# Two layers on one core: earlier chunk loads around a second weight, transposes in place of products, and constant products in TensorE's first gaps

## The reference

```
h = rms_norm(x, g)                          # both layers begin so
p = h @ w_in_2                              # 2048 x 6448
wd, ad, gd, a, b = the narrow parts of p    # 304 columns: "LoRA" inputs, decay and beta
...
L = where(strict, (k_beta @ k.T) * gamma, 0)        # 8 heads x 4 chunks of 64 tokens: 32 of 64x64
sol = triangular_solve(L + eye, [v_beta, k_beta * exp(g)])
```

## Time and profile before

| | |
|---|---|
| median of 3 runs | 2945.02 us |
| the profiled execution | 2943.11 us, its span 2941.4 us |
| PE (matmul) busy | 2876.3 us, 98% |
| PEld (weight load) | 2480.6 us, 84% |
| DVE (VectorE) busy | 1600.7 us, 54% |
| ACT (ScalarE) busy | 1167.7 us, 40% |
| POOL (GpSimd) busy | 58.6 us, 2% |
| DMA | 501.12 MB, mean 170 GB/s |

### The profile page before, as it was taken

How to read it: one execution, slowest core, us unless ns; L and a number is a source line. 1 busy time by engine, 2 the same in 40 slices (tenths; PEclk the granted TensorE clock), 3 DMA queues, 4 the chain that set the end, 5 groups by cost and what they waited for, 6 DMA issues and landing times.

```text
span 2941.4 us, 41822 instructions
## 1 busy us (share of the span) xinstructions
PE 2876.3 (98%) x18274; PEld 2480.6 (84%) x18274; DVE 1600.7 (54%) x1325; ACT 1167.7 (40%) x958; POOL 58.6 (2%) x124
## 2 busy tenths in 40 slices
PE   8999999999999999999998999988899999999998
PEld 7999888888888888888888989988788888888887
DVE  5657555444554455444447657875555445544445
ACT  4345444334443333333335343423344343333333
POOL 0000000000000000002002000000000000000000
PEclk9999999999999999999999999999899999999999
DMA  6555555656555555555565445300255555655554
GB/s 216 163 164 180 161 168 189 197 187 195 186 190 186 185 191 191 188 186 192 194 209 171 158 132 170 101 4 32 86 167 191 186 187 189 195 185 186 198 189 171
DMA packets 257411, 501.12 MB, mean 170 GB/s; under 512 B 12256, under 2 KB 17707, under 8 KB 256891
## 3 DMA queue, kind: packets, MB, share of 16 engines
q1 hardware_dynamic: 257275, 499.06, 52.3%
HBM read 496.74 MB, written 2.10 MB: 170 GB/s over the span
## 4 chain that ended last, share of the span: by engine, by line
PE 94%; DVE 4%; ACT 1%; DMA 1%; issue 0%; SPq 0%; DVEq 0%; ACTq 0%
PE psum L696 23%; PE psum L698 23%; PE psum L697 23%; PE psum L681 5%; PE psum L683 5%; PE psum L684 5%; PE psum L1130 2%; DVE weight_lo L1899 1%; PE psum L747 1%; PE psum L1011 0%; PE psum L642 0%; DMA weight_raw<-in_w_in 0%; ACT weight_hi L1427 0%; PE psum L1017 0%; PE psum L1023 0%; PE psum L996 0%
## 5 line engine op out<-in xcount | busy, mean ns | idle before, releaser
L1899 DVE TENSOR_TENSOR weight_lo<-weight_raw,weight_hi 128x2048 fp32r<-128x2048 f32 x460 | 1054.0, 2292 | 1109.3 <-ACT weight_hi L1427 1108.7
L1427 ACT ACTIVATE weight_hi<-weight_raw 128x2048 fp32r<-128x2048 f32 x460 | 881.4, 1916 | 1509.8 <-PE psum L698 1211.7
L696 PE MATMUL psum<-weight_hi,h_both 128*128 128x512 f32 x1856 | 724.9, 391 | 0.0
L698 PE MATMUL psum<-weight_hi,h_both 128*128 128x512 f32 x1856 | 722.5, 389 | 0.0
L697 PE MATMUL psum<-weight_lo,h_both 128*128 128x512 f32 x1856 | 722.1, 389 | 0.0
L681 PE MATMUL psum<-h_both,weight_hi 128*128 128x256 f32 x1408 | 403.9, 287 | 18.4 <-DVE weight_lo L1899 18.3
L698 PEld LDWEIGHTS psum<-weight_hi,h_both 128*128 128x128 f32 x1856 | 348.3, 188 | 72.8
L697 PEld LDWEIGHTS psum<-weight_lo,h_both 128*128 128x128 f32 x1856 | 348.5, 188 | 71.4
L696 PEld LDWEIGHTS psum<-weight_hi,h_both 128*128 128x128 f32 x1856 | 348.4, 188 | 71.3
L683 PE MATMUL psum<-h_both,weight_lo 128*128 128x256 f32 x1408 | 400.6, 285 | 0.0
L684 PE MATMUL psum<-h_both,weight_hi 128*128 128x256 f32 x1408 | 400.4, 284 | 0.0
(11 more groups left out here) (525 smaller groups left out, 2228.5 us busy)
## 6 DMA issues: line engine op xcount, KB each, us to landing
weight_raw<-in_w_in SPq DMA_DIRECT2D x144, 1024.0 KB, 5.3
weight_raw<-in_w_ffn_in SPq DMA_DIRECT2D x88, 1024.0 KB, 5.0
weight_raw<-in_w_ffn_out SPq DMA_DIRECT2D x44, 1024.0 KB, 5.1
weight_raw<-in_ffn_w_gate SPq DMA_DIRECT2D x44, 1024.0 KB, 5.1
weight_raw<-in_ffn_w_up SPq DMA_DIRECT2D x44, 1024.0 KB, 5.2
weight_raw<-in_ffn_w_down SPq DMA_DIRECT2D x44, 1024.0 KB, 5.1
weight_raw<-in_w_out SPq DMA_DIRECT2D x32, 1024.0 KB, 5.1
weight_raw<-in_w_branch_rnn SPq DMA_DIRECT2D x8, 1024.0 KB, 5.1
```

What stands on the lines that cost most here:

```text
L696: mm(acc[:, t, :], xh[:, c], wh[:, k, :], start=(start and k == 0), stop=False, skip_group_check=True)
L698: last = mm(acc[:, t, :], xl[:, c], wh[:, k, :], start=False, stop=(stop and k == CK - 1), skip_group_check=True)
L1427: A(hi[j % g.hi][:], raw[j % g.ring][:], ACT.Copy).then_inc(hi_ready, 1)
L1899: V.tensor_tensor(lo[r][:], raw[r][:], hi[j % g.hi][:].bitcast(F32), ALU.subtract).then_inc(lo_ready, 1)
```

## The change

It has three parts.

1. **Loads of the second layer's start.** Chunks 4 and 5 now stand on SP ahead of the wait for `n_sq`; `w_lora` comes in two halves, with chunk 6 between them, and chunk 7 behind. ScalarE rounds chunks 4 to 6 ahead of the first half of `w_lora` and waits for all four of its loads at once.
2. **The inverse.** For k below 4 the product that made the transpose is gone, and VectorE makes the transpose from `x` by `V.transpose` (`chunk_turn`). The first transpose is made in the same way, in the loop of the RWKV state, in place of six masking operations.
3. **The start.** A function `keep_clock` multiplies the constants `ident` and `ones`, five products a time, into a bank that is not in use: ahead of `first_turn(0)`, between the two turns, and ahead of product 0.

```diff
-            load(in2, 0, 0, 4)
+            def load_lora(p0, p1):
+                k = slice(4 * p0, 4 * p1)
+                sp.dma_start(w_lora[:, k, 0:288], w_in2[:, k, 3072:N_RWKV]).then_inc(S("lora_w_landed"), 16)
+                sp.dma_start(w_lora[:, k, 288:LC], w_in2[:, k, 6432:6448]).then_inc(S("lora_w_landed"), 16)
+
+            load(in2, 0, 0, 6)
             sp.wait_ge(n_sq, 16)
-            sp.dma_start(w_lora[:, :, 0:288], w_in2[:, :, 3072:N_RWKV]).then_inc(S("lora_w_landed"), 16)
-            sp.dma_start(w_lora[:, :, 288:LC], w_in2[:, :, 6432:6448]).then_inc(S("lora_w_landed"), 16)
-            load(in2, 0, 4)
+            load_lora(0, 2)
+            load(in2, 0, 6, 7)
+            load_lora(2, 4)
+            load(in2, 0, 7)
...
+            def keep_clock(n):
+                for k in range(n):
+                    mm(bank(2)[:, 0:P], ident[:], ones[:], start=True, stop=True, skip_group_check=True)
+
+            keep_clock(5)
             first_turn(0)
+            keep_clock(5)
             first_turn(1)
+            keep_clock(5)
...
             def chunk_x(k, b):
                 pe.wait_ge(S("gd_z_out"), 2 * k + b + 1)
-                of_chunks(bank(4 + 2 * b), lambda r, u: xt_gc[r, u, :], lambda r, u: z_gc[r, u, :], 8, 8 * b)
-                of_chunks(bank(5 + 2 * b), lambda r, u: z_gc[r, u, :], lambda r, u: xt_gc[r, u, :], 8, 8 * b).then_inc(S("gd_x"), 1)
+                pe.wait_ge(S("gd_xt_out"), 2 * k + b + 1)
+                last = of_chunks(bank(4 + 2 * b), lambda r, u: xt_gc[r, u, :], lambda r, u: z_gc[r, u, :], 8, 8 * b)
+                if k == 4:
+                    last = of_chunks(bank(5 + 2 * b), lambda r, u: z_gc[r, u, :], lambda r, u: xt_gc[r, u, :], 8, 8 * b)
+                last.then_inc(S("gd_x"), 1)
...
-            chunks(in2, 0, 4, 6)
-            act.wait_ge(S("lora_w_landed"), 32)
+            chunks(in2, 0, 4, 7)
+            act.wait_ge(S("lora_w_landed"), 64)
             act.wait_ge(*at_step("x_rescaled"))
-            lora_high(0, 1)
-            chunks(in2, 0, 6, 7)
-            lora_high(1, 3)
+            lora_high(0, 2)
             chunks(in2, 0, 7, 8)
-            lora_high(3, 4)
+            lora_high(2, 4)
...
+            def chunk_turn(k, b):
+                u = slice(8 * b, 8 * b + 8)
+                dve.wait_ge(S("gd_x_out"), 2 * k + 2 + b + 1)
+                V.transpose(xt_gc[:, u, :], x_gc[:, u, :]).then_inc(S("gd_xt_out"), 1)
...
-                if g == 3:
-                    dve.wait_ge(S("gd_nt_out"), 2)
-                    gd_begin(xt_gc, nt_g, low0_t_c, 0)
+                if g >= 2:
+                    chunk_turn(-1, g - 2)
...
-            dve.wait_ge(S("gd_nt_out"), 4)
-            settle(gd_begin(xt_gc, nt_g, low0_t_c, 1))
...
             def chunk_z(k):
                 for b in range(2):
                     u = slice(8 * b, 8 * b + 8)
+                    if b and k:
+                        chunk_turn(k - 1, 1)
                     dve.wait_ge(S("gd_z"), 2 * k + b + 1)
...
-                    for o, x in enumerate((x_gc, xt_gc)):
-                        last = V.tensor_tensor(x[:, u, :], x[:, u, :], bank(4 + 2 * b + o).rearrange("p (u n) -> p u n", u=8), ALU.add)
-                    last.then_inc(S("gd_x_out"), 1)
+                    for o, x in enumerate((x_gc, xt_gc) if k == 4 else (x_gc,)):
+                        V.tensor_tensor(x[:, u, :], x[:, u, :], bank(4 + 2 * b + o).rearrange("p (u n) -> p u n", u=8),
+                                        ALU.add).then_inc(S("gd_xt_out" if o else "gd_x_out"), 1)
+                if k < 4:
+                    chunk_turn(k, 0)
```

More of the change, by code:

```diff
@@ L1338, in _ @@
                 pe.wait_ge(S("gd_z_low_out"), b + 1)
+                pe.wait_ge(S("gd_xt_out"), 10 + b + 1)
                 for u in range(8):
@@ L2678, in _ @@
             chunk_x(4)
-            dve.wait_ge(S("gd_x_out"), 12)
+            dve.wait_ge(S("gd_xt_out"), 12)
             V.memset(head_rstd[UP, 0:1], 0.0).then_inc(S("gd_xt_made"), 1)
```

## The result

The changed kernel took 2920.99 us, the median of 4 runs (2918.75 to 2923.88), against 2945.14 us for the kernel before on the same chip (4 runs, 2941.74 to 2945.82). The ratio is 0.9921, with a 95% interval of 0.9904 to 0.9938: faster, by less than 1%. The forecast was 2921.6 us, in a range of 2915.5 to 2930.

What follows compares the result with a forecast made beforehand. TensorE held 94% of the chain, so gains come where it stands still, runs at its low clock or has less work. 13.4 + 7.8 + 2.2 = 23.4 us, from the median 2945.02, gave 2921.6 us, range 2915.5 to 2930.

Steps and rivals of the forecast that it cites:

- Part 1, 13.4 us: Second layer's start: earlier chunk loads remove TensorE's 11.70 us wait and the low clock behind it; 13.4 us gained.
- a wait moves into the `w_lora` loads: Second layer's loads: chunk 7 lands 5 us late, TensorE stands before product 7; gain 18.4 us, 2926.6 us; chance 0.10.
- part 1 does nothing: Second layer's loads: SP's queue does not reach chunk 4 earlier; gain 10.0 us, 2935.0 us; chance 0.01.
- Part 2, 7.8 us: Inverse: two groups of 16 matmuls leave each of four steps on TensorE's way; 7.8 us gained, bounds 4 and 11.
- the part named as open: Inverse: TensorE's clock around the waits may stay low longer or hold; bounds of the gain 4 and 11 us.
- the inverse gives half or nothing: Inverse: half, by the clock, 2925.4 us, chance 0.12; nothing, as VectorE and ScalarE set its pace, 2929.4 us, chance 0.03.
- Part 3, 2.2 us with an upper bound of 2.6: Start: constant products raise the clock earlier, so product 0's matmuls run faster; 2.2 us gained, bounds −0.25 and 2.6.
- The rival of the clock: Start: product 0 stays at the low clock, as turns may not count as busy; 2924.0 us; chance 0.20.

Runs made afterwards that it cites:

- e3: Kernel before with only the constant products at the start added: 2941.81 us, ratio 0.999.
- e8: The changed kernel run once more, with nothing altered: 2920.77 us, ratio 0.9919.
- e9: Changed kernel plus 12 constant products ahead of the first of four waits in the inverse alone: 2918.08 us, ratio 0.9909.
- e1: Kernel before with only the new order of loads on SP and of ScalarE's work: 2934.22 us, ratio 0.9956.
- e2: Kernel before with only the change to the inverse: 2933.85 us, ratio 0.996.
- e4: Changed kernel with each constant product of `keep_clock` replaced by two transposes of `ones`: 2919.68 us, ratio 0.9915.
- e7: Changed kernel plus 12, 7, 7 and 10 constant products ahead of four waits in the inverse: 2914.43 us, ratio 0.99.
- e10: Changed kernel plus 6, 3, 3 and 5 constant products ahead of four waits in the inverse: 2917.28 us, ratio 0.9906.
- e6: Changed kernel with only the last of the three batches of constant products, that ahead of product 0: 2918.93 us, ratio 0.9921.

## Why the prediction came out right

The time was right to 0.6 us, and the mechanism of each part came out; that it was right so closely is in part luck. In the profiled execution part 3 and the inverse gave 3.3 us more than predicted, and two losses that aren't in the sum, at the gate product and behind the inverse, took 2.1. The other trace of the same kernel gained 18.2 us in all.

- **Part 1, 13.4 us: measured 13.15**, in all nine traces that have it. Every step came as it was written: chunk 4 at 1576.23 + 3.17 (the start's gain up to there) = 1579.4, predicted 1579.5; no wait ahead of product 4; 0.80 us ahead of product 5, predicted 0.8; `w_lora` hidden. Product 5 started at 1587.59 + 3.17 = 1590.76, predicted 1590.9. The 0.25 us too much come from two small things: the sum took 1604.26, the start of ScalarE's copy, for the start of product 5 before, which was at 1604.00; and behind the wait the second matmul follows the first after 0.22 us in place of 0.12. The rivals that a wait moves into the `w_lora` loads, and that part 1 does nothing, are excluded.
- **Part 2, 7.8 us: measured 8.1 alone, 8.8 to 10.1 with the others (without fills).** The removed work is there as counted: 3.88 − 2.02 = 1.86 us in step 0. The waits kept their length. What lies above it is the clock, the part named as open: in the changed kernel L1344 took 2.13 us for 3.78, and L1030 0.70 for 1.19, 2.1 of the 2.3 us. The waits stand at other moments, and so the low level covers other work. That the inverse gives half or nothing is refuted.
- **Part 3, 2.2 us with an upper bound of 2.6: measured 3.1 in the profiled execution.** The sum "they would save 28 × 0.093 = 2.6 us, at most" counted only the matmuls inside product 0. Here the clock rose inside turn 0 already, which took 1.40 us for 1.97 and released VectorE and ScalarE 0.57 us earlier, so that product 0 itself started at 14.30 and not at 14.86. But that was not the usual case. Of the eight traces with three batches only this one and e3 (1.50 us) have a short turn 0; in the other six it took 1.97, product 0 started between 14.81 and 14.91, and 1.1 to 2.6 us were gained by product 3, inside the predicted bounds. The lower ones, e8 and e9 (1.1 to 1.2), are those in which the clock fell again within product 0. The one trace of before isn't typical either: without constant products the turn of piece 2 started at 23.26, at 22.44 in e1 and 22.28 in e2, a mean of 22.66; with three batches at 20.04 to 22.17, a mean of 20.93. That makes this part 1.7 us between the means. By medians e3 has 3.7, with an interval of 0.3 to 5.6 (0.0001 and 0.0019 of 2945.5).
- **The rival of the clock** had as its first ground that the turns may not count as busy. e4 shows that they do. In all eight traces with three batches the clock was up by the first or second matmul of product 0.
- **Not in the sum: −1.5 us at the gate product**, −1.5 in e9, −4.5 and −4.6 in e8 and e1, and 0 in the rest. It is in none of the three traces in which the loads are as before, and in four of the nine with the new loads; if the loads had nothing to do with it, such a split would come about one time in four. The place has moved by 13 to 17 us, but no experiment was made on it, and why the clock falls there stays open. The −0.6 behind the inverse wasn't in the sum either.

The sum of the profile is 3.2 + 13.15 − 1.5 + 10.1 − 0.6 = 24.4 us, where 23.4 were predicted.

## What to carry to other kernels

A load that stands in a queue behind another one's wait is late by that wait, however free its own buffer is: look for a stretch in which DMA moves nothing while an engine waits for a chunk, and move the load, not the work. Where TensorE waits for another engine for some microseconds, the work behind it may run at the low clock; constant products into a free bank cost nothing there. In the traces here they gained 5.2 us when they covered nearly the whole of four waits that follow one another, and at most 0.6 with one of the four covered or each half covered (e7 against e9 and e10, one trace of each). And a term that hangs on when the clock rises shouldn't be read off a single profile: here it moved by 1 to 2 us between executions of one kernel, while the times with the new loads agreed to 0.01 us from trace to trace.

## What was not expected of the hardware

- A batch of 10 transposes of constants raised TensorE's clock as well as 5 products did (e4: turn 1 in 1.09 us in place of 1.97).
- The granted clock fell to 0.50 while TensorE was busy for 10.00 of 10 us and 5.00 of 5 us in the records (1694 to 1709 of the changed kernel), for 10 us in e1. It also fell within product 0 in e8, at 16 us, and in e9, with the product's matmuls following each other 0.12 us apart.
- The profile's clock rows say 1.00 from 14 to 16 us in e6, where matmuls of 256 columns follow each other in 0.21 us. In the start the spacing is what can be read.
